# Half of a product-key expert layer moved from gathered rows to dense matmuls with gate tables

## The reference, cut to what matters

```
P_HEADS, N_KEYS, P_TOPK, P_HALF = 8, 128, 16, 128      # 128*128 = 16384 experts
def peer(h, w_query, sub_keys, u_tab, v_tab):          # u_tab, v_tab [16384, 1024]
    q = (xb @ w_query).reshape(TOKEN_BLOCK, P_HEADS, 2, P_HALF)
    s = einsum('thpk,hpnk->thpn', q, sub_keys)
    sv, si = top_k(s, 16)
    cand = sv[:, :, 0, :, None] + sv[:, :, 1, None, :]         # 256 per head
    cidx = si[:, :, 0, :, None] * N_KEYS + si[:, :, 1, None, :]
    fv, fpos = top_k(cand, 16)
    eidx = take_along_axis(cidx, fpos);  g = softmax(fv)
    act = gelu(einsum('td,thkd->thk', xb, u_tab[eidx]))
    return einsum('thk,thkd->td', g * act, v_tab[eidx])
x = x + g2 * peer(h2, ...);  return rmsnorm_2(x, final_g)
```

## Time and profile before

| what | value |
|---|---|
| median of three runs | 2700.69 us (2699.71 to 2701.6) |
| span of the profiled execution | 2699.1 us |
| time of that execution outside its span | not listed |
| TensorE, VectorE, ScalarE, GpSimd busy | 80%, 62%, 29%, 23% |
| moved by DMA | 692.66 MB, mean 257 GB/s |
| queries begin | 1355.8 us |
| 512 gathers issued and dotted | 1376.6 to 2687 us |

### The profile page before, as it was taken

How to read it: one execution, slowest core, us unless ns; L and a number is a source line. 1 busy time by engine, 2 the same in 40 slices (tenths; PEclk the granted TensorE clock), 3 DMA queues, 4 the chain that set the end, 5 groups by cost and what they waited for, 6 DMA issues and landing times.

```text
span 2699.1 us, 20390 instructions
## 1 busy us (share of the span) xinstructions
PE 2168.8 (80%) x6274; PEld 1025.0 (38%) x6274; DVE 1675.7 (62%) x3651; ACT 794.1 (29%) x2184; POOL 626.4 (23%) x543
## 2 busy tenths in 40 slices
PE   6999999999999999999989666656565665556665
PEld 3454555444444444454478222223222222222221
DVE  5444454220114505234679888889889988889876
ACT  2022364110000002222333334334333334334332
POOL 0000000000000000000024444444444444444442
PEclk9999999999999999999999777888877788888778
DMA  9621010211236511211169999999999999999996
GB/s 371 241 102 63 32 63 32 80 76 62 89 129 258 210 62 65 76 47 63 47 236 370 407 427 427 427 427 427 427 427 427 427 426 425 428 425 420 421 423 275
DMA packets 85545, 692.66 MB, mean 257 GB/s; under 512 B 9504, under 2 KB 9504, under 8 KB 10688
## 3 DMA queue, kind: packets, MB, share of 16 engines
q0 software_dynamic: 77520, 590.33, 52.7%
q1 hardware_dynamic: 7200, 96.47, 9.4%
q10 hardware_dynamic: 720, 4.62, 0.4%
HBM read 689.28 MB, written 2.10 MB: 256 GB/s over the span
## 4 chain that ended last, share of the span: by engine, by line
PE 48%; DMA 29%; DVE 16%; issue 5%; POOL 1%; ACT 1%; POOLq 0%; DVEq 0%; ACTq 0%
PE PS L562 22%; DMA arena<-in_peer_uv,arena 20%; PE PS L592 8%; DMA ring<-in_peer_uv,arena 8%; DVE arena L1960 4%; PE PS L1104 4%; PE PS L1150 3%; DVE arena L1948 3%; PE PS L747 2%; PE PS L1468 2%; DVE ring L1948 1%; PE PS L767 1%; PE PS L756 1%; DMA arena<-in_ada 1%; PE PS L1125 1%
## 5 line engine op out<-in xcount | busy, mean ns | idle before, releaser
L1468 PE MATMUL PS<-arena 128*128 128x512 f32 x768 | 476.8, 771 | 320.1 <-ACT arena L1637 300.3
L2040 POOL DMA_INDIRECT arena<-in_peer_uv,arena x340 | 410.0, 1206 | 925.9 <-DVE arena L1930 461.5
L1948 DVE CUSTOM_DVE_ANT_0 arena<-arena 128x1024 f32<-128x1024 f32 x340 | 414.0, 1226 | 101.0 <-DMA arena<-in_peer_uv,arena 98.4
L1468 PEld LDWEIGHTS PS<-arena 128*128 128x128 f32 x768 | 177.1, 244 | 604.0 <-ACT arena L1637 415.7
L1468 PE MATMUL PS<-ring,arena 128*128 128x512 f32 x428 | 259.4, 755 | 138.9 <-ACT arena L1637 130.2
L562 PE MATMUL PS<-arena,ring 128*128 128x512 f32 x832 | 359.2, 593 | 2.1 <-issue 0.8
L1630 ACT ACTIVATE arena<-arena 128x1 f32<-128x1 f32 x512 | 103.2, 202 | 776.3 <-DVE arena L1948 775.5
L562 PE MATMUL PS<-hT,ring 128*128 128x256 f32 (+1 forms) x928 | 301.5, 486 | 7.0 <-ACT arena L1655 4.2
L2040 POOL DMA_INDIRECT ring<-in_peer_uv,arena x172 | 201.6, 1172 | 214.5 <-DVE arena L1960 159.4
L1948 DVE CUSTOM_DVE_ANT_0 ring<-ring,arena 128x1024 f32<-128x1024 f32 x172 | 209.1, 1226 | 45.2 <-DMA ring<-in_peer_uv,arena 42.8
L562 PEld LDWEIGHTS PS<-arena,ring 128*128 128x128 f32 x832 | 157.0, 190 | 203.2 <-issue 201.9
(11 more groups left out here) (321 smaller groups left out, 2231.4 us busy)
## 6 DMA issues: line engine op xcount, KB each, us to landing
ring<-in_wstream SPq DMA_DIRECT2D x45, 2048.0 KB, 7.5
arena<-in_ada POOLq DMA_DIRECT2D x24, 2048.0 KB, 8.7
arena<-in_peer_uv,arena POOLq DMA_INDIRECT x340, 17.6
ring<-in_peer_uv,arena POOLq DMA_INDIRECT x172, 17.6
xT<-in_xT POOLq DMA_DIRECT2D x1, 2048.0 KB, 18.5
arena<-in_alibi ACTq DMA_DIRECT2D x1, 2048.0 KB, 14.4
result<-arena SPq DMA_DIRECT2D x3, 512.0 KB, 7.7
arena<-in_subkeys ACTq DMA_DIRECT2D x1, 1024.0 KB, 4.8
```

The source lines that it names most:

```text
L1468: ins = pe.matmul(bank(6 + b), diag[:, k % NDIAG, :], rows[slot_of(n)][:, D + b * 512:D + (b + 1) * 512], start=opens, stop=closes)
L1948: dve.tensor_tensor_reduce(u, u, h2tok[t % 2], 1.0, 0.0, ALU.mult, ALU.add, dots[:, e:e + 1]).then_inc(dot_ok, 1)
L2040: pool.indirect_dma_start(rows[j], None, ap["peer_uv"], bass.IndirectOffsetOnAxis(ap=eidx[:, t, e:e + 1], axis=0)).then_inc(landed[j], 16)
```

## The change

The first two token blocks (`NGT = 2`, `NPICK` = 256) are still gathered. For the last two (256 tokens) every expert is computed:

- Gate tables. The picks of the dense tokens (`selij`: both indices of each, and the gate) are turned so that a pick is a partition (`turn_picks`, `copy_picks`). For each token a matmul of two one-hot matrices, the first scaled with the gate (`first_one_hots` on ScalarE as Square and Relu, or on VectorE by `made_on_dve`; `second_one_hots` on VectorE), gives its 128x128 table of gates (`gate_tables`, four tokens to a group g, 64 groups). ScalarE copies it to `gstage` (`copy_gate_table`) and stores it to memory, 16 blocks of 1 MiB; SP loads them back in another order (`load_gates`, pieces of 512 bytes).
- Dense experts. A chunk c is the 128 experts with second index c. `dense_dots` (8 matmuls of 128x256) multiplies a block of a turned u table (`u_turned`, 512 KiB) with the tokens, `dense_gelu` is ScalarE's, `dense_weights` VectorE's product with the gates, and 4 matmuls of 128x512 with the 128 value rows (`load_values`, 512 KiB, rows 1 MiB apart) add the result in PSUM. The first 24 chunks' dots (`AHEAD`) are made early.
- Order. 24 beats b come first. A beat has one head's selection for the dense tokens (b under 16), two or three gathered picks (56 in all, all on TensorE), and from beat 8 on four gate-table groups; in beats 7 to 14 one or two pairs of chunks are dotted as well. Then comes the dense loop over 128 chunks with picks 56 to 255 beside it, all values on VectorE, tied to each other by `pick_at` (1.73 picks a chunk).
- Buffers. Gathers have 3 buffers up to pick 14, 6 up to pick 36, then 7. `last` works on PSUM for the dense blocks, and three of the four blocks are finished at the end.

Its core (the other edits rename buffers and semaphores, or give the heads a common list `JOBS`):

```diff
-NPICK = T * NSLOT
-EARLY = 36
+NGT = 2
+NPICK = NGT * NSLOT
+NCHUNK = 128
+AHEAD = 24
+NBEAT = 24
-SLOTS, FREED_BY_SCORES, _order = [], {}, [0, 1, 2, 3, 4, 5]
+SLOTS, _order = [], [0, 1, 2]
 for _n in range(NPICK):
+    if _n == 14:
+        _order = [3, 4, 5] + _order
+    if _n == 36:
+        _order = [6] + _order
+def made_on_dve(g):
+    return g % 4 == 3 if g < 32 else g % 2 == 1
+def dense_pair(b, q):
+    m = 3 * (b - 7) // 2 + q
+    return m + 1 if 7 <= b < 15 and m < 3 * (b - 6) // 2 else 0
+def pick_at(chunk):
+    return NEARLY + (max(0, chunk) * 173) // 100
 # SyncE
+            sp.wait_ge(g_pe, 64)
+            load_values(0)
+            for q in range(2):
+                sp.wait_ge(g_stored[q], 16 * 8)
+            load_gates(0)
...
+            for c in range(NCHUNK):
+                if c + AHEAD + 3 < NCHUNK:
+                    sp.wait_ge(s_done, c + AHEAD + 1)
+                    sp.dma_start(ubuf[c % 3], ap["u_turned"][c + AHEAD + 3]).then_inc(u_loaded[c % 3], 16)
+                if c + 3 < NCHUNK:
+                    sp.wait_ge(d_done, c + 1)
+                    load_values(c + 3)
 # TensorE
+            def dense_dots(j):
+                pe.wait_ge(u_loaded[j % 3], 16 * (j // 3 + 1))
+                if j % 2 == 0 and j >= 4:
+                    pe.wait_ge(s_ev, j // 2 - 1)
+                for k in range(KD):
+                    ins = pe.matmul(dense_bank(j), ubuf[j % 3][:, tile(k)], hT[:, k, 256:512], start=(k == 0), stop=(k == KD - 1))
+                ins.then_inc(s_done, 1)
+            for b in range(6, NBEAT):
+                values(beat_picks(b - 1))
+                if b >= 7:
+                    for q in range(4):
+                        if q < 2 and dense_pair(b, q):
+                            dense_dots(2 * dense_pair(b, q) - 2)
+                            dense_dots(2 * dense_pair(b, q) - 1)
+                        if b in (8, 16) and q == 0:
+                            turn_picks(b // 8 - 1)
+                        if b >= 8:
+                            gate_tables(4 * (b - 8) + q)
+            for c in range(NCHUNK):
+                if c + AHEAD < NCHUNK:
+                    dense_dots(c + AHEAD)
+                pe.wait_ge(w_ok, c // 2 + 1)
+                pe.wait_ge(vt_loaded[c % 3], 16 * (c // 3 + 1))
+                for td in range(2):
+                    for half in range(2):
+                        ins = pe.matmul(bank(2 + 2 * td + half), weights_of(c)[:, tile(td)], vbuf[c % 3][:, half * 512:half * 512 + 512],
+                                        start=(c == 0), stop=(c == NCHUNK - 1))
+                ins.then_inc(d_done, 1)
 # ScalarE
+                if b >= 7:
+                    for q in range(4):
+                        if q < 2 and dense_pair(b, q):
+                            dense_gelu(dense_pair(b, q) - 1)
+                        if b >= 8:
+                            g = 4 * (b - 8) + q
+                            if not made_on_dve(g):
+                                first_one_hots(g)
+                            if g >= 1:
+                                copy_gate_table(g - 1)
+            for n in range(NEARLY, NPICK):
+                while m < NCHUNK // 2 and pick_at(2 * m + 1 - AHEAD) <= n:
+                    dense_gelu(m)
+                    m += 1
+                weights(n)
 # VectorE
+            for n in range(NEARLY, NPICK):
+                dot(n)
+                while done < min(n + 1 - lag_of(n), NPICK):
+                    value(done)
+                    done += 1
+                while m < NCHUNK // 2 and n >= max(NEARLY + 2 + m, pick_at(2 * m + 1 - 14)):
+                    dense_weights(m)
+                    m += 1
```

More of the change, by code:

```diff
@@ L1422, in turn, with key_scores, values @@
                 return ins
+            def key_scores(m):
+                half, h = PAIRS[m]
+                pe.wait_ge(evac, EV0["pq"] + 2 * m + 2)
+                if m >= 2:
+                    pe.wait_ge(pk_ev, m - 1)
+                for t in range(2):
+                    for c in range(2):
+                        ins = pe.matmul(PS[:, 2 + m % 2, tile(2 * t + c)], pqt[:, (2 * m + c) % 4, tile(t)], skw[:, 2 * h + c, :],
+                                        start=True, stop=True)
+                ins.then_inc(sk_done, 1)
+            def values(picks):
+                for n in picks:
+                    k = PE_BEFORE[n]
+                    pe.wait_ge(diag_ok, k + 1)
+                    if n == 0:
+                        pe.wait_ge(g2_ev, 1)
+                    for b in range(2):
+                        ins = pe.matmul(bank(6 + b), diag[:, k % NDIAG, :], rows[slot_of(n)][:, D + b * 512:D + (b + 1) * 512],
+                                        start=(n == 0), stop=(n == NEARLY - 1))
+                    ins.then_inc(v_pe, 1)
             for i, (half, c) in enumerate(QUERIES):
-                g = BLOCK0["pq"] + c // 4
-                if half == 0 and c % 4 == 0:
+                g = BLOCK0["pq"] + i // 8
+                if i % 8 == 0:
                     block_arrived(pe, g)
@@ new lines, in _ @@
+                if i == 6:
+                    pe.wait_ge(tt_ev, 1)
+                    for b in range(2):
+                        ins = turn(hT, 1, b, 6 + b)
+                    ins.then_inc(tt_pe, 1)
+                if i == 9:
+                    pe.wait_ge(tt_ev, 2)
+                    for k in range(KD):
+                        ins = pe.matmul(PS[:, 6 + k // 4, tile(k % 4)], modc2[:, 40 + k:41 + k].to_broadcast([P, P]), ident,
+                                        start=True, stop=True)
+                    ins.then_inc(g2_pe, 1)
@@ L1678, in _ @@
+            for t in range(1, T):
+                act.wait_ge(fin_ms, t + 1)
+                act.activation(ssf[t][:, 0:1], ssf[t][:, 0:1], ACT.Sqrt).then_inc(fin_rt, 1)
         @block.vector
@@ L1991, in _ @@
-            done = 0
-            for n in range(NPICK):
+                    own(dve.reciprocal(ss[:, 2:3], ss[:, 0:1]))
+                    dve.scalar_tensor_tensor(out=acc[t], in0=acc[t], scalar=ss[:, 2:3], in1=fgrow, op0=ALU.mult, op1=ALU.mult)\
+                       .then_inc(fin_ok, 1)
+            job(0)
+            gated = 0
+            for b in range(NBEAT):
+                if b < 16:
+                    k = JOB[2 + b // 8, b % 8]
+                    job(k, gated)
+                    gated = k
+                picks = beat_picks(b)
+                dot(picks[0])
+                if b in (16, 19, 23):
+                    pick_gates(gated)
+                for n in picks[1:]:
+                    dot(n)
+                if b in GATHER_JOB_AT:
+                    hd = GATHER_JOB_AT[b]
+                    k = JOB[hd // PH, hd % PH]
+                    if b < 16:
+                        job(k, gated)
+                    else:
+                        job(k)
+                    gated = k
+                if b >= 8:
+                    for q in range(4):
+                        g = 4 * (b - 8) + q
+                        if q % 2 == 0:
+                            second_one_hots(g // 2)
+                        if made_on_dve(g):
+                            first_one_hots(g)
@@ L2003, in _ @@
-                if t > 0 and e in LAST_AT:
-                    last(t - 1, LAST_AT.index(e))
-            for n in range(done, NPICK):
-                if not on_pe(n):
-                    value(n)
-            for step in range(5):
-                last(T - 1, step)
+                while m < NCHUNK // 2 and n >= max(NEARLY + 2 + m, pick_at(2 * m + 1 - 14)):
+                    dense_weights(m)
+                    m += 1
+                for back, piece in ((13, pick_keys), (11, pick_pairs), (9, pick_experts), (5, pick_gates)):
+                    hd = (n + back) // PK
+                    if (n + back) % PK == 0 and 5 <= hd < NGT * PH:
+                        piece(JOB[hd // PH, hd % PH])
@@ L2012, in _ @@
+                if n >= NSLOT and n - NSLOT in LAST_AT:
+                    last(0, LAST_AT.index(n - NSLOT))
+            for n in range(done, NPICK):
+                value(n)
+            while m < NCHUNK // 2:
+                dense_weights(m)
+                m += 1
+            for t, step in ((1, 0), (1, 1), (1, 2), (1, 3), (2, 0), (2, 1), (2, 2), (3, 0), (3, 1), (3, 2), (2, 3), (3, 3)):
+                last(t, step)
         @block.gpsimd
```

631 lines of the change are left out of this document (381 added, 250 removed).

## The result

The changed kernel takes 2861.1 us (median of four runs, 2854.9 to 2869.3) against 2700.2 for the kernel before: 1.0598 times as long, 95% interval 1.0578 to 1.0619. The forecast said slower, and by 25 us; it is 161 us. 2861 lies outside the range of 2650 to 2795. The profiled execution took 2863.4 us, its span is 2861.3, so 2.1 us lie around the span.

A forecast was written before the change was run, and what follows sets the result against it. Full transfers were taken to bound the old kernel, transfers and TensorE nearly equally the new loop. Restart at 1883, loop 816 to last landing 2699, tail 24, plus 1.6: 2725 us; range 2650 to 2795.

The forecast's parts named there:

- The loop: Dense loop from 1883: transfers 789 us and TensorE 803 nearly equal, TensorE not kept waiting; 816 us, last landing 2699.
- the 803: Dense loop: TensorE's own work on dots and values at full clock, 803 us with a head start of one chunk.
- the tail: After the last landing: dot and two values 4, three token blocks 17.5, result 2.5, together 24 us.
- The gate loads' term: Dense loop: transfer of 16 gate blocks, 39 us at 427 GB/s.
- The factor 1.034: Dense loop: slowdown for gathers mixed with SP's blocks, bounds 1.00 and 1.12, giving 816 us.
- The beats: Before the loop: beats 8 to 14 take 211 us with 19 for clock, beat 15 17, beats 16 to 23 118.
- the restart: Between beats and dense loop: last table stored and first block loaded, from 1876 to 1883, bounds 1850 and 1930.
- Rival 1: Beats 8 to 14: hand-overs hidden, 123 us instead of 211, time 2637, half of it 2681; chance 0.27.
- Rival 2: Dense loop: full transfer rate holds in the mix, 27 us less, time 2698; chance 0.14.
- Rival 3: Dense loop: value and gate blocks come slowly; a quarter lost gives 2790, a tenth 2747; chance 0.13.
- Rival 4: Beats 8 to 14: TensorE goes cold, 64 us instead of 19, time 2770; chance 0.12.
- The wait that I had called likeliest: Dense loop: VectorE's selections hold up dots with only seven buffers, 11 selections of 9 us, at worst 100 us.

The follow-up runs named there:

- The combined kernel: Changed kernel plus 8 KiB gate loads, contiguous value rows, 1.60 picks a chunk and all first one-hots on VectorE: 2719.4 us, 1.0064 of the kernel before.
- the layout: Changed kernel with gate tables stored in pieces of 512 bytes and loaded in pieces of 8 KiB: 2803.6 us, 1.0392 of the kernel before.
- the reorder: Changed kernel with ScalarE making a group's first one-hots before the pair's GELU instead of after it: 2825.4 us, 1.0458 of the kernel before.

## Why the prediction was wrong in size

**The loop, 84 us: the step that failed.** "three buffers of each leave some 17 us against a landing under 12, so TensorE is not kept waiting". I had named SyncE's one order of loads and its waits as the danger, and then checked it with the landing of a u or value block (8.9 and 9.3 us, so that part was right). The gate block is in the same list: it lands in 22.7 us, and the issue behind it is held 14.6. With a landing of 8.9 behind it that is more than the 17. TensorE stands still for 80 us in the loop, and its matmuls take 27 us more than the 803. Without the gate loads loop and tail take 826 us, 806 of it TensorE's work, so the 803 was right to 3 us (and 13.7 lie behind TensorE where the tail had 24). The gate loads' term was 39 us for 16; it is 101 for 14. About 58 of that is gone with large pieces in the load, and what is left, 43, is near their bytes (14 x 2.46 = 34). The factor 1.034 for the mixed rate stood for this and was too small: 426/390 = 1.09 with the small pieces; 426/411 = 1.04 without.

On the held issue the Trainium skill, Perfetto Trace Analysis, section "DMA Instruction — HWDGE (DVE, Sync)", says that the recorded time of such an issue covers its wait for the descriptor unit and the generation of its descriptors. The 14.59 us on the short u load can be such a wait, behind the 2064 packets of a gate block (from the 28,896 that q1 lacks without 14 loads), and they are absent when the block has large pieces ((76944 - 46224)/16 = 1920 packets less for each). But by the page the generation of the gate block's own descriptors would lie in its own record, and that is 0.43 us here; which unit holds the next issue, no run here shows.

**The tail** is inside the 84 us. I counted 24 us from the last landing; the last dot starts at 2812.0, and from there it is 49. TensorE had 13 chunks left at the last gather's issue and about 11 when it landed: 200 picks at 1.73 a chunk end at chunk 116. I had read 1.73 and not multiplied it out. TensorE is the last there and works with hardly a gap (0.6 us), so these chunks are its own work at another time and no cost of their own; the loss is that the gathers shared the transfers with the other loads before, and left them idle at the end (share 0.48 in the last 61 us). At 1.60 the time is 20 us less, by shorter waits for u as well as by the shorter tail.

**The beats, 54 us.** The mechanism held line for line: ScalarE between pair and group, idle 3.53 against 3.6. In beats 8 to 14 TensorE stands still for 67 us (59 foreseen) and is busy for 160 (133 + 19). The sizes that were off: the copy, taken as 0.55 from an in-order copy of 128x512, is 1.03 because it writes every 16th word, worth 17 us; the restart, 20.7 us for 7, since the last store and then the first gate load (of the slow kind) stand ahead of the first weights; and the clock. I charged 19 us to beats 8 to 14, "since the pair runs unbroken for 10 us", and nothing like it to beats 16 to 23 beyond 14 us each. The window shows 0.79, and with three of four one-hots on VectorE 32 us of matmul time come back in gate tables and values alone.

**The rivals.** Rival 1 (hand-overs hidden) did not happen. With all first one-hots on VectorE the loop begins 83 us earlier, near its price of 88, but that agreement is luck: the 88 was for beats 8 to 14 alone, from 211 to 123, and these go from 227 to 162. Rival 2 is out: 390 GB/s. Rival 3 named the right loads and the wrong loss. It put "value and gate blocks" together at a tenth or a quarter; the value half costs at most some 8 us, and taking the gate loads out of SyncE's list gives back 48 us, a place and not a rate. The rule I cited there, the Trainium skill, DMA: Bandwidth & Descriptors, section "Latency and other measured facts", gave an estimate of 5 to 47 us for the value rows; 8, with intervals that overlap, is its lowest end or nothing. The page's copies run between HBM tensors with 16 KiB in each partition; here rows of 4 KiB go into SBUF. Rival 4 was part of the answer at well under half its size: 28 us over the work at full clock in beats 8 to 14 (160 - 133) where it had 64 and the forecast 19. The wait that I had called likeliest, for VectorE's selections, did not come up: from the first dense values on TensorE waits for u and value blocks alone. None of them alone reaches 2861; loop, tail and beats all went wrong to the same side, and I had let none of the combinations into the range.

**The direction** rested on two counts: few gathers pass before the dense loop begins, and then TensorE's 803 us cannot be passed. The second holds: the dense values take 812 us even without the gate loads. That the change could not have been faster is not shown. The combined kernel is 0.6% slower, but its end is set by the pace of the picks and not by TensorE.

**Open.** TensorE's account for the 59.5 us by which the layout shortens the span is 47 of waiting, 9 of faster matmuls and 4 of an earlier start; how the waiting divides between the held issue and slower landings isn't separated, since the two go together in that run. The restart (16 us of waiting in the best version too) stays: every block that is loaded holds a part of each of the tables, so none can be loaded before the last is stored, and no other division of the tables was tried. Nor was a pace between 1.60 and 1.73 in the combined kernel.

## What to carry to other kernels

Where one queue issues several kinds of loads in one order, check the buffer slack against the slowest kind, landing and hold of the next issue, and not against the kind that is needed. If a tensor must be turned through memory, put the small pieces on the side where the DMA engines are idle. When two streams are tied by a ratio, multiply it out to the end: a stream that finishes early leaves the other alone with its tail. And set the ratio again when one of the streams has become faster.

## What the hardware showed that was not expected

- A load of 1 MiB in 512-byte pieces took 4.5 us of the 16 DMA engines against 2.5 in 8 KiB pieces, 22.7 us to land, and made the next issue on its queue last 3.3 to 18.1 us (14.59 in the rows shown) instead of 0.33. Issued from ScalarE's queue, such a load took a median of 59.5 us to land, and its issue up to 7.7 us.
- ScalarE's copy of 128x512 out of PSUM takes 1.03 us when it writes every 16th word and 0.58 when it writes in order.
- 128 rows of 4 KiB that lie 1 MiB apart land in 9.3 us, side by side in 9.2.
- In the beats TensorE's idle time that was removed brought matmul time with it: 38 us of idle and 32 us of matmul time with three of four one-hots on VectorE, the granted clock going from 0.79 to 0.86; 25 and 12 with the reorder, 0.79 to 0.84.
